# Spreading the cumulated decays of a state-space mixer over the partitions: one product over 128 rows in place of two over 64

## The reference, cut to what matters

```python
cum = jnp.cumsum(lac, axis=1)                    # per head, inside a chunk of 128 tokens
decay = jnp.exp(jnp.where(causal, cum[:, :, None] - cum[:, None], -jnp.inf))
xdt = xc * dtc[..., None]
cb = jnp.einsum('blgn,bsgn->blsg', cc, bc)
y = jnp.einsum('blsgr,bsgrp->blgrp', cb[..., None] * decay, xdt)
y = y + jnp.einsum('blgn,bgrpn->blgrp', cc, state) * jnp.exp(cum)[..., None]
tail = jnp.exp(cum[:, -1:] - cum)
state = state * jnp.exp(cum[:, -1])[..., None, None] + jnp.einsum(...)
```

## Time and profile before

| what | value |
|---|---|
| median of 3 runs | 2023.86 us (2022.34 to 2026.95) |
| the profiled execution's own time | 2024.04 us |
| its span, first to last instruction | 2022.3 us |
| TensorE busy | 1813.3 us, 90% |
| VectorE busy | 1259.3 us, 62% |
| ScalarE busy | 782.1 us, 39% |
| GpSimd busy | 414.5 us, 20% |
| mean granted TensorE clock | 0.946 |

### The profile page before, as it was taken

One profiled execution on the slowest core, in us unless ns is written; L12 is line 12 of the kernel. 1 busy time (PEld: TensorE's weight loads), 2 busy tenths in 40 slices (PEclk: granted clock), 3 DMA queues, 4 the chain that ended last, 5 costly groups with the idle time before them and its releaser, 6 DMA issues. The chain is left out here.

```text
span 2022.3 us, 21708 instructions
## 1 busy us (share of the span) xinstructions
PE 1813.3 (90%) x8200; PEld 1456.5 (72%) x8200; DVE 1259.3 (62%) x1664; ACT 782.1 (39%) x1167; POOL 414.5 (20%) x368
## 2 busy tenths in 40 slices
PE   5899999999978989999977997787899889999997
PEld 4677777777755868787855776565678868888886
DVE  6867877887757564757446779766456454434342
ACT  5333344334424352525244423344444343223232
POOL 0533564355442000000006024400021020000001
PEclk9999999999978989999988999898899889999999
DMA  3212222212102212222212322111223224333332
GB/s 109 68 52 63 55 64 71 63 52 63 63 13 55 82 43 72 63 84 63 84 42 58 91 65 68 43 30 28 84 84 89 58 63 115 94 97 101 94 95 72
DMA packets 252190, 139.21 MB, mean 69 GB/s; under 512 B 25965, under 2 KB 246550, under 8 KB 252086
## 3 DMA queue, kind: packets, MB, share of 16 engines
q1 hardware_dynamic: 252086, 137.82, 24.0%
HBM read 135.70 MB, written 2.10 MB: 68 GB/s over the span
## 5 line engine op out<-in xcount | busy, mean ns | idle before, releaser
L65 PE MATMUL stream<-u_lo,weights_hi 128*128 128x512 f32 (+2 forms) x1312 | 533.2, 406 | 41.3 <-DVE weights_lo L133 19.1
L133 DVE TENSOR_TENSOR weights_lo<-weights_raw,weights_hi 128x1024 fp32r<-128x1024 f32 (+4 forms) x266 | 342.0, 1286 | 300.7 <-ACT weights_hi L123 300.4
L66 PE MATMUL stream<-u_hi,weights_lo 128*128 128x512 f32 (+2 forms) x1312 | 518.9, 396 | 0.0
L67 PE MATMUL stream<-u_hi,weights_hi 128*128 128x512 f32 (+2 forms) x1312 | 518.3, 395 | 0.0
L123 ACT ACTIVATE weights_hi<-weights_raw 128x1024 fp32r<-128x1024 f32 (+4 forms) x266 | 268.1, 1009 | 470.2 <-PE stream L67 421.1
L65 PEld LDWEIGHTS stream<-u_lo,weights_hi 128*128 128x128 f32 (+2 forms) x1312 | 250.2, 191 | 117.0 <-DVE weights_lo L133 27.8
L67 PEld LDWEIGHTS stream<-u_hi,weights_hi 128*128 128x128 f32 (+2 forms) x1312 | 249.9, 190 | 55.7 <-issue 0.3
L66 PEld LDWEIGHTS stream<-u_hi,weights_lo 128*128 128x128 f32 (+2 forms) x1312 | 250.8, 191 | 54.1 <-issue 3.2
L203 POOL COPY h_sum_of_squares<-h_squares 128x512 f32<-128x512 f32 x5 | 3.2, 649 | 852.8 <-ACT h_squares L191 852.8
L65 PE MATMUL stream<-mlp_a_lo,weights_hi 128*128 128x512 f32 x256 | 100.2, 391 | 0.0
L67 PE MATMUL stream<-mlp_a_hi,weights_hi 128*128 128x512 f32 x256 | 99.7, 389 | 0.0
(11 more groups left out here) (497 smaller groups left out, 3363.9 us busy)
## 6 DMA issues: line engine op xcount, KB each, us to landing
weights_raw<-in_w_mlp_dram SPq DMA_DIRECT2D x64, 512.0 KB, 4.0
weights_raw<-in_ssd_w_in_dram SPq DMA_DIRECT2D x48, 512.0 KB, 3.9
weights_raw<-in_gla_w_in_dram SPq DMA_DIRECT2D x40, 512.0 KB, 3.8
weights_raw<-in_w_in_dram SPq DMA_DIRECT2D x29, 512.0 KB, 3.8
weights_raw<-in_ssd_w_out_dram SPq DMA_DIRECT2D x16, 512.0 KB, 3.5
weights_raw<-in_gla_w_out_dram SPq DMA_DIRECT2D x16, 512.0 KB, 3.4
weights_raw<-in_w_out_dram SPq DMA_DIRECT2D x8, 512.0 KB, 4.0
weights_raw<-in_w_xkv_dram SPq DMA_DIRECT2D x8, 512.0 KB, 4.1
```

The lines of the kernel that those rows point to most:

```text
L65: pe.matmul(out, lh, rl, start=first, stop=False, skip_group_check=skip)
L66: pe.matmul(out, ll, rh, start=False, stop=False, skip_group_check=skip)
L67: return pe.matmul(out, lh, rh, start=False, stop=last, skip_group_check=skip)
L133: dve.tensor_tensor(lo, raw_view(c, n), hi.bitcast(F32), ALU.subtract).then_inc(c.w_split, 1)
```

## The change

The rounded part and the rest of `cum` are put on the two halves of the partitions of one tile, `cum_parts` (128 by 512): ScalarE writes partitions 0 to 63, VectorE writes partitions 64 to 127. The selecting operand gets 128 rows, so that one product sums both parts. It is no longer made by `affine_select`: once, at the start, GpSimd adds the two halves of the identity matrix into `head_pick` (128 by 64), and for each group two copies with a repeating input spread its columns over `head_spot`.

```diff
-        cum_h = sb("cum_hi", [64, T], F32R)
-        cum_l = sb("cum_lo", [64, T], F32R)
+        cum_parts = sb("cum_parts", [P, T], F32R)
+        pick = sb("head_pick", [P, 64])
...
+                    pool.wait_ge(s_const, 1)
+                    pool.tensor_tensor(pick[:, :], c.ident[:, 0:64], c.ident[:, 64:P], ALU.add).then_inc(s_const, 1)
                     pool.memset(go[:, :], 1.0).then_inc(s_go, 1)
...
-        pick = mb("head_pick", [64, 4, P], F32R)
-        s_pick = sem("head_pick_ready")
+        spot = mb("head_spot", [P, 2, 2, P], F32R)
+        s_spot = sem("head_spot_ready")
...
                         if g:
                             pool.wait_ge(s_e, 4 * g)
-                        for p in range(2):
-                            for d in range(2):
-                                pool.affine_select(
-                                    out=pick[:, 2 * p + d, :].rearrange("r (h m) -> r h m", h=2),
-                                    in_=c.ones[0:64, :].rearrange("r (h m) -> r h m", h=2),
-                                    compare_op=ALU.is_equal, fill=0.0, base=-(HPG * g + 2 * p + SH * d),
-                                    pattern=[[-1, 2], [0, 64]], channel_multiplier=1).then_inc(s_pick, 1)
+                        for d in range(2):
+                            a = HPG * g + SH * d
+                            pool.tensor_copy(spot[:, d, :, :].rearrange("r p (h m) -> r (p h) m", h=2),
+                                             spread(pick[:, a:a + HPG], HD)).then_inc(s_spot, 1)
...
                     if e == 0:
-                        pe.wait_ge(s_pick, 4 * g + 4)
+                        pe.wait_ge(s_spot, 2 * g + 2)
                         pe.wait_ge(s_decay, 4 * g + 4)
...
-                    w = pick[:, e, :]
-                    pe.matmul(dst[:, :], w, cum_h[:, :], start=True, stop=False)
-                    pe.matmul(dst[:, :], w, cum_l[:, :], start=False, stop=True).then_inc(s_e, 1)
+                    pe.matmul(dst[:, :], spot[:, d, p, :], cum_parts[:, :], start=True, stop=True).then_inc(s_e, 1)
...
-                        act.activation(cum_h[:, :], cum[:, :], ACT.Copy).then_inc(s_a, 1)
+                        act.activation(cum_parts[0:64, :], cum[:, :], ACT.Copy).then_inc(s_a, 1)
...
-                        dve.tensor_tensor(cum_l[:, :], cum[:, :], cum_h[:, :].bitcast(F32), ALU.subtract)\
+                        dve.tensor_tensor(cum_parts[64:P, :], cum[:, :], cum_parts[0:64, :].bitcast(F32), ALU.subtract)\
                            .then_inc(s_v, 1)
```

## The result

| what | before | after |
|---|---|---|
| median, same chip | 2025.4 us of 6 (2022.34 to 2027.87) | 2008.41 us of 6 (2006.31 to 2016.07) |
| ratio | | 0.9922 [0.9902, 0.9942] |
| profiled execution's own time, span | 2024.04, 2022.3 us | 2006.31, 2004.6 us |
| granted clock | 0.946 | 0.951 |

What follows compares the result with a forecast made beforehand. The SSD loop was taken as bound by a ring of VectorE with GpSimd, TensorE, and a ScalarE-VectorE-GpSimd chain; 1.6 + 1.3 + 2.7 = 5.6 us off 2024.04 gave 2018.4 us, range 2014.5 to 2022.7.

Steps and rivals of the forecast that it cites:

- the prediction's own sign: SSD loop: the forecast is wrong if the period falls by much more than 0.6 us, the ring then being misread.
- the ring: SSD loop period of 67.69 us: VectorE with GpSimd, then TensorE (slots 5 and 6), then a ScalarE, VectorE, GpSimd, ScalarE chain.
- The second product of each spread: TensorE, slot 5 spread: removing one product saves 0.23 us in each of groups 0 to 6, 1.6 us.
- That the sum now runs over 128 rows and not 64 costs nothing: TensorE's spread products: the first product of either height takes 0.50 us, so the greater height adds nothing.
- The selecting operand: GpSimd: two copies, 0.62 us, replace four selections, 1.00 us; 0.38 us in each of groups 1 to 7, 2.7 us.
- Since VectorE's `weights_lo` was held until that end: VectorE at 340.08: held until GpSimd's run ends, so it gets through 0.38 us earlier when that run does.
- my first rival: VectorE gets in at the next border of GpSimd's run: 7.8 us, with the last group 9.1, time 2014.9; chance 0.16.
- Nothing in the instructions differs between the two places: Argument for the first rival: `weights_lo` got in early at 78.07 (1.50 us) but not at 340.08 (3.42 us).
- Its price was capped at line 877: First rival: once TensorE's line 877 no longer waits, its own saving counts, 0.20 + 4 × 0.23 = 1.12 us a group.
- The parts add up: The sum: the separate terms were simply added, 1.6 + 1.3 + 2.7 = 5.6 us.
- The last group: Last group's spreads lie on the chain, TensorE's clock being low: three steps of 0.43 us saved, 1.3 us.

Runs made afterwards that it cites:

- e12: Kernel before, with both products of each spread over 128 rows and the selections still on 64 partitions; 2021.33 us.
- e8: Changed kernel plus a GpSimd memset of 256 elements on partitions 0 to 63, between the copies and the first `la_steps`; 2019.55 us.
- e3: Changed kernel, but with two products over 64 rows in each spread as before, so GpSimd's copies alone; 2033.59 us.
- e2: Changed kernel with its one product over the upper 64 rows alone, leaving out the rest part of the cumulated decays; 2021.22 us.
- e7: Changed kernel plus a GpSimd memset of 256 elements on all 128 partitions, between the copies and the first `la_steps`; 2013.59 us.
- e6: Changed kernel plus a wait ahead of GpSimd's third `la_steps` that never waits, in effect a repeat; 2007.57 us, ratio 0.992.
- e10: Kernel before, with its four selections on all 128 partitions and the products still reading 64 rows; 2027.35 us.

## Why the prediction was wrong

By the prediction's own sign, a period that falls by much more than 0.6 us (it fell by 1.96), something in its reading of the ring was wrong. It was not the ring itself but what its pieces cost.

*The ring* held. e12 shortened TensorE's piece alone, by 0.43 us, and the period fell by 0.43; e8 lengthened VectorE's piece alone, by 1.25 us against after, and the period grew by 1.27.

*The second product of each spread.* 0.23 us was right: from e12 (two of 128 rows) to after (one) six periods of H to R lose 1.4 us, 0.23 each, and from e3 to e2 (two and one of 64) it is 0.22 each.

*"That the sum now runs over 128 rows and not 64 costs nothing"* is the first step that failed, in sign. On the H to R piece the height was worth 0.43 us a period by e12 against before, 2.6 us over six, and 0.45 by after against e2. On the R to H piece it decides whether TensorE comes in time: e2, the changed kernel with 64 rows, is 11.6 us longer over six periods than after, 9.0 of it there. I compared two products of 0.50 us, a 64-row one and the 128-row one behind the pair, and took them for two heights at the same price. Both stood at a change of height. The stream product took 0.50 us from its 64-row neighbour, and takes 0.40 behind a 128-row one; at the first product of the pair the price stood in the step ahead of it, 0.98 us against 0.81 (e12). A row of a 128-row product between its like was two lines below, 0.39.

*The selecting operand.* The copies were priced nearly right: 0.70 us for the pair from start to start, 333.32 to 334.02, against 0.62 forecast. *"Since VectorE's `weights_lo` was held until that end"* is the second step that failed. VectorE was held till the end because the selections wrote 64 partitions; on 128 it gets in at the next border. That is 1.3 us a period at R, 7.8 us in six, and not the 0.30 that the copies' length gives. This was my first rival, with its reason wrong and its price too small. Its reason was another point of the run; but e7 and e8 make the request at the same point, and differ. "Nothing in the instructions differs between the two places" overlooked that the selections stand right ahead of the run at 340.08 and not at 78.07. Its price was capped at line 877, taken to be TensorE's limit. But each spread had become shorter by more than the 0.23 us that this limit was made of. In e8, where VectorE is held as before, TensorE's wait there is up from 0.20 us to 1.64, and the forecast had at most 0.89 (0.20 + 3 x 0.23):

```profile
345.04 1.96 PE L876 MATMUL q<-ssd_exp_cum,ones 128*128 128x512 f32 x4 [1.64 <-DVE ssd_cb L1111]
```

In the changed kernel TensorE still waits 0.40 us there: the limit did not bite.

*The parts add up* was assumed and is false. The six periods change by -4.1 us with TensorE's part while VectorE is held (e8, its memset included), by +5.8 with the copies alone (e3), and by -11.8 with both. Without TensorE's part the early entry is lost again, since VectorE's next operations meet the next `la_steps`.

*The last group.* Forecast were 1.3 us, besides the 0.38 for its `weights_lo`; measured 3.94. From the last R to the first exponential it is 1.55 us (581.42 - 543.13 = 38.29 before, 569.91 - 533.17 = 36.74 after). Some 1.1 of it is the entry at R: e8, the changed kernel with VectorE held, has 37.88. The rest shows in ScalarE's and TensorE's timelines after, and in the granted clock of two windows of after:

```profile
569.91 0.60 ACT L962 ACTIVATE ssd_exp_cum<-q 128x512 f32<-128x512 f32 x1 [4.23 <-PE q L806]
572.48 0.60 ACT L962 ACTIVATE ssd_exp_cum<-q 128x512 f32<-128x512 f32 x1 [1.98 <-PE q L806]
...
571.97 0.47 PE L806 MATMUL q<-ssd_cum_parts,ssd_head_spot 128*128 128x512 f32 x1
...
572.00:580.00 8.00, 5.95 (x25) 4.89 (x25) 2.71 (x5) 6.25 (x7) 3.28 (x3) 0.79 0.01 2
580.00:590.00 10.00, 6.17 (x22) 3.48 (x20) 5.62 (x9) 2.46 (x4) 4.09 (x3) 1.00 0.19 52
```

The same windows view of before, where the products of the last spreads stand at 580 to 592 us:

```profile
580.00:590.00 10.00, 8.66 (x30) 6.23 (x29) 2.14 (x4) 5.11 (x6) 2.27 (x3) 0.51 0.00 0
```

The second exponential starts 2.57 us after the first, where it was 4.01 (585.43 less 581.42), and the spread ahead of it takes 0.47 us where such products took 0.75. TensorE was at the lower of its two levels (1.2 and 2.4 GHz) nearly all of 580 to 590 us before (0.51); after, the level rose during these products. In e8, which has the products of after, the granted clock is 0.50 between the exponentials as it was before, and they lie 2.99 us apart. So about 1.0 of these 1.4 us comes without the clock and 0.4 with it. Removed products and height can't be told apart in it (e12, with as many products as before, has 2.50 us, at a clock of 0.67), and the changed kernel itself has 3.36 us in e6.

The Trainium skill's page "SBUF — State Buffer", section "SBUF: two separate sides", says that the shared port is locked for one whole instruction. It stood beside my first rival, which got 0.16. By the runs it describes GpSimd work on 128 partitions (1.36 and 1.42 us, e7 and e10) and not that with a 64-partition instruction in the run (3.37 and 3.42, e8 and before).

What stays open: why an instruction on 64 partitions has this effect on the ones behind it, and how long GpSimd must be idle for it to end. In the kernel before it was idle for 2.36 and 1.99 us between the run of 338 to 342 us and the next `la_steps`, at 347.80, which VectorE's operations already get in between.

## What to carry to other kernels

When two products of half height stand between full-height ones, stack their halves on the partitions: it saves the product and also the two changes of height, which here were worth twice the product. When VectorE's operation is held across several borders of GpSimd's work, look for a GpSimd instruction on half the partitions earlier in that run before trying to make the run shorter. A stall that goes on one engine is kept as a gain only if the engine that feeds the next step has slack; read the waits behind it before adding up the parts.

## What the runs showed of the hardware

- A 64-row product between 128-row ones costs time at both borders, about 0.2 us each: 1.98 us against 1.59 for the same products (before, e12), 1.75 against 1.36 with one product (e2, after).
- A 64-partition instruction of GpSimd keeps VectorE's two-input operation out until GpSimd's unbroken run ends: 3.37 us (e8) against 1.36 (e7), two kernels that differ only in the partitions of a memset of 0.31 us. Later in the same period, after idle times of GpSimd of 2.36 us and less, the effect is gone (before, `weights_lo` of 367.11: 1.82 us).
- A selection of 128 elements takes 0.25 us on 64 or on 128 partitions, and a rounding copy of 256 elements with repeating input 0.35 us.
